# A one-core decoder trunk: overflow table and spill list moved into the expert loop, first experts in loop order

## What is computed

```python
def hier_moe(x, w_rg, b_rg, w_re, b_re, w_e1, w_e3, w_e2):
    g_idx = jnp.argmax(g_logits, axis=-1)                      # 1 of 4 groups
    top_v, top_i = lax.top_k(e_sel, TOP_K)                     # 2 of 8 experts in it
    top_w = jax.nn.softmax(top_v, axis=-1) * g_gate
    ...
        a = jnp.einsum('nd,edf->nef', xf, w_e1[g])
        b = jnp.einsum('nd,edf->nef', xf, w_e3[g])
        hid = jax.nn.silu(a) * b * gates[:, g, :, None]
        y = y + jnp.einsum('nef,efd->nd', hid, w_e2[g])
```

## Time and profile before

| | |
|---|---|
| median of 3 runs | 1172.28 us (1171.71 to 1172.39) |
| the profiled execution: own time | 1172.48 us |
| the profiled execution: span from first to last instruction | 1170.7 us |
| mean granted TensorE clock over the span | 0.954 of full |
| PE matmul busy | 1059.8 us, 91% |
| DVE, ACT, POOL busy | 645.6, 448.4, 196.9 us |
| moved by DMA | 203.04 MB |

### The profile page before, as it was taken

The page is one execution under the profiler, slowest core; times in us unless marked ns, Lnnn a source line. Parts: engine busy times, 40 slices in busy tenths (PEclk is TensorE's granted clock), DMA queues, the critical chain, the costliest instruction groups (busy, mean ns, idle before and its releaser), DMA issues. The chain is left out here.

```text
span 1170.7 us, 14132 instructions
## 1 busy us (share of the span) xinstructions
PE 1059.8 (91%) x5307; PEld 857.2 (73%) x5307; DVE 645.6 (55%) x1208; ACT 448.4 (38%) x777; POOL 196.9 (17%) x144
## 2 busy tenths in 40 slices
PE   2899999798999999998875999957999999999966
PEld 2899998697887799994542878745777777777722
DVE  5823735225644720004644115777888888888527
ACT  4522101204322522122421102255677777777413
POOL 3401211100000212100000300205422222222100
PEclk9999999999999999999986999967999999999978
DMA  9501111225000631106206101159999999999275
GB/s 331 146 19 36 40 55 36 90 73 200 11 1 30 227 140 54 37 8 280 108 1 257 67 1 73 55 192 386 340 382 392 379 386 394 371 400 363 89 303 185
DMA packets 55019, 203.04 MB, mean 173 GB/s; under 512 B 10534, under 2 KB 19231, under 8 KB 41383
## 3 DMA queue, kind: packets, MB, share of 16 engines
q1 hardware_dynamic: 44167, 181.61, 42.2%
q0 software_dynamic: 10784, 20.52, 4.8%
HBM read 189.52 MB, written 28.36 MB: 186 GB/s over the span
## 5 line engine op out<-in xcount | busy, mean ns | idle before, releaser
L500 PE MATMUL bank<-regA_r,regW_r 128*128 128x352 f32 (+1 forms) x456 | 149.6, 328 | 0.0
L499 PE MATMUL bank<-regA_r,regW_r 128*128 128x352 f32 (+1 forms) x456 | 149.3, 327 | 0.0
L498 PE MATMUL bank<-expert_w_r,regS_r 128*128 128x512 f32 x256 | 105.6, 413 | 2.6 <-DVE regS_r L2113 2.6
L334 POOL TENSOR_TENSOR regW_r<-regW,regW_r 128x1024 fp32r<-128x1024 f32 x19 | 47.2, 2487 | 330.5 <-ACT regW_r L328 330.5
L1416 ACT ACTIVATE regY_r<-expert_w 128x1024 fp32r<-128x1024 f32 x88 | 91.6, 1061 | 3.6 <-DMA expert_w<-in_we 3.6
L498 PE MATMUL bank<-regY_r,regW_r 128*128 128x352 f32 (+1 forms) x264 | 87.9, 333 | 0.5 <-ACT regB L1134 0.5
L2096 DVE TENSOR_TENSOR expert_w_r<-expert_w,regY_r 128x1024 fp32r<-128x1024 f32 x69 | 82.7, 1218 | 7.7 <-ACT regY_r L1416 7.7
L499 PEld LDWEIGHTS bank<-regA_r,regW_r 128*128 128x128 f32 x456 | 86.4, 190 | 0.4
L500 PEld LDWEIGHTS bank<-regA_r,regW_r 128*128 128x128 f32 x456 | 86.0, 189 | 0.0
L500 PE MATMUL bank<-regY_r,regA_r 128*128 128x512 f32 (+1 forms) x216 | 84.3, 390 | 0.0
L499 PE MATMUL bank<-regY_r,regB_r 128*128 128x512 f32 (+1 forms) x216 | 84.2, 390 | 0.0
(11 more groups left out here) (332 smaller groups left out, 2348.8 us busy)
## 6 DMA issues: line engine op xcount, KB each, us to landing
expert_w<-in_we SPq DMA_DIRECT2D x96, 1024.0 KB, 8.1
regW<-in_wbc SPq DMA_DIRECT2D x11, 512.0 KB, 3.6
regA<-in_kct SPq DMA_DIRECT2D x5, 1024.0 KB, 6.6
regY<-in_cache_mem_v SPq DMA_DIRECT2D x5, 1024.0 KB, 9.3
regS<-in_x_prompt SPq DMA_DIRECT2D x8, 512.0 KB, 9.0
regY<-in_xt SPq DMA_DIRECT2D x8, 512.0 KB, 8.5
regX<-in_x_prompt SPq DMA_DIRECT2D x8, 512.0 KB, 6.5
regW<-in_wq SPq DMA_DIRECT2D x8, 512.0 KB, 3.5
```

The lines of the kernel that those rows point to most:

```text
L334: eng.tensor_tensor(lo, raw, hi.bitcast(F32), ALU.subtract).then_inc(w_lo[name], 1)
L498: nc.tensor.matmul(out, stays[0], moves[1], start=first, stop=False)
L499: nc.tensor.matmul(out, stays[1], moves[0], start=False, stop=False)
L500: ins = nc.tensor.matmul(out, stays[0], moves[0], start=False, stop=last)
```

## The change

Seven edits, all around the start of the expert loop. (1) `place_in_table(0)` leaves tile 4, (1) and (2) leave the place behind `idx`; the three run at the ends of experts 5, 8 and 11 on DVE. (2) POOL's 18 table writes go two by two into experts 12 to 20. (3) `spill_list()` is cut into six pieces, at the ends of experts 16 to 26; `gates()` goes from expert 2 to 14. Their scratch moves to tiles that the loop doesn't overwrite. (4) On PE, `tokens(1)` is issued in the middle of `ab(0)`. (5) ACT rounds the down weights of expert 0 ahead of the tokens of expert 1. (6) A SiLU of one column is put behind the two Exp of the gates, so that the table for SiLU is loaded there. (7) SP issues piece 4 ahead of its wait, and then waits for three gathers instead of two.

```diff
-            def ab(e):
+            def ab(e, midway=None):
...
+                    if c == 2 and midway is not None:
+                        midway()
...
             for e in range(NE):
-                ab(e)
-                if e == 0:
-                    tokens(1)
+                ab(e, (lambda: tokens(1)) if e == 0 else None)
...
-            for p in range(2, 4):
+            for p in range(2, 5):
                 part_load(p)
-            for s in range(2):
-                sp.wait_ge(m_g[s], 16)
-            for p in range(4, 3 * NE):
+            sp.wait_ge(m_g[1], 16)
+            sp.wait_ge(m_g[0], 32)
+            for p in range(5, 3 * NE):
                 part_load(p)
...
+            nc.scalar.activation(small[:, 2:3], small[:, 0:1], ACT.Silu)
...
             for e in range(2):
                 act.wait_ge(m_tx, e + 1)
                 for q in range(2):
                     token_hi(e, q)
+                if e == 0:
+                    part_to_hi("down", 0, 0)
...
-                if t == 4:
-                    place_in_table(0)
...
-            place_in_table(1)
-            place_in_table(2)
...
-                if e == 0:
-                    spill_list()
-                if e == 2:
+                if e in (5, 8, 11):
+                    place_in_table((e - 5) // 3)
+                if e == 14:
                     gates()
+                if e == 16:
+                    spill_counts()
+                if e == 18:
+                    spill_ends((1, 2))
+                if e == 20:
+                    spill_ends((4, 8, 16))
+                if e == 22:
+                    spill_experts()
+                if e == 24:
+                    spill_before()
+                if e == 26:
+                    spill_columns()
...
-            g.wait_ge(s_plc, 1)
-            for t in range(GT):
-                for c in range(2):
-                    place_rows(t, c)
...
-            for t in range(GT, NT):
-                if t % GT == 0:
-                    g.wait_ge(s_plc, t // GT + 1)
-                for c in range(2):
-                    place_rows(t, c)
             for e in range(NE):
                 if e + 4 < NE:
                     rows_in(e + 4)
                 if e >= 1:
                     rows_out(e - 1)
+                if 12 <= e < 12 + NT:
+                    g.wait_ge(s_plc, (e - 12) // GT + 1)
+                    for c in range(2):
+                        place_rows(e - 12, c)
```

## The result

The changed kernel took **1161.38 us**, the median of 4 executions (1156.52 to 1162.57), against 1172.3 (1171.71 to 1172.39) for the kernel before beside it: ratio 0.990, 95% interval 0.9872 to 0.9929. In the course of the study more executions came together, on several chips: 10 of the changed kernel with a median of 1160.5 (1156.17 to 1162.57), and 40 of the kernel before with 1172.3 (1168.08 to 1177.39), 11.8 apart. The forecast was 1161.1, a gain of 11.2.

The account below looks back on a forecast made before the run. PE, busy for 91% of the span, was taken as the bound, with only waits and slow clock to win. Terms 1.08 + 1.26 + 2.10 + 0.84 + 2.41 + 1.89 + 1.60 make 11.2; 1172.3 less that is 1161.1 us, range 1159 to 1163.5.

Parts of the forecast that it names:

- Edit 1, router, 1.08: Router of tile 5: without the table piece beside tile 4, PE's wait goes, winning 1.08 us, at least 0.
- Edit 1, `token_lo(0)`, 1.26: Before the first up product: earlier low halves let PE start at 790.8 instead of 792.06, winning 1.26 us.
- Edits 4 and 5, 2.10: At `tokens(2)`: with `tokens(1)` inside `ab(0)`, PE's wait for `token_lo` goes, winning 2.10 us.
- Edit 6, 0.84: At `hidden(0)`: loading SiLU's table early wins 0.84 of the 1.08 us wait; 0.24 stays.
- Clock, 2.41 and 1.60: Over `ab(1)` and `ab(2)`: without the waits ahead the clock should not fall, winning 2.41 and 1.60 us.
- Edit 3, 1.89: At `hidden(1)`: with the spill list out of DVE's way, PE's wait for `hid(1)` goes, winning 1.89 us.
- The loop at 0: In the expert loop: the moved DVE pieces and POOL table writes fit into slack and cost PE 0 us.
- Loads late: First experts: late weight loads or gather 3 stop PE once or twice by 1 to 2 us; gain 7, chance 0.20.
- Table writes: In the loop: 18 table writes cost the DMA engines 4.9 us; if that reached PE, gain 6.3; chance 0.07.
- loop bound by DMA: In the loop: DMA engines already bind, PE only by coincidence; 2.2 us slower, 1174.5 us; chance 0.04.
- DVE one for one: In the loop: DVE's moved pieces reach PE in full, 11.2 less 11.5, no change at 1172.6 us; chance 0.03.
- SiLU's load not hidden: Before the first `token_hi`: a table load of twice 1.28 us passes ACT's idle time by 0.5; 1161.6 us; chance 0.03.

Follow-up runs that it names:

- the experiment with the late load: Changed kernel without the early one-column SiLU, so SiLU's table loads before the loop's first SiLU again: 1159.43 us, ratio 0.9885 to the kernel before.
- 2.64 in expert 16: PE's wait in the changed kernel with all six spill-list pieces together at the end of expert 16: 1163.97 us, ratio 0.9921 to the kernel before.

## Why the prediction was right, and where it was not

The forecast held: 1161.1 against 1161.38, inside the likeliest case's own range of 1159 to 1163.5. That it is right to 0.3 us is partly luck, for ten executions span 6.4 us, and by the starts of the same instructions these two traces are 12.6 us apart (1.19, 11.36 and 0.01), 0.7 of it by when the clock rose in `ab(0)`. Its steps held unevenly.

- **Edit 1, router, 1.08: right.** The wait is gone, and back at 1.09 when the piece is put back. The part to `tokens(0)` became 1.19 shorter (48.07 to 46.88), which contains also the loss of 0.51 below; the wait is 1.08 of it, and a last router that is 0.3 us quicker in this execution is most of the rest.
- **Edit 1, `token_lo(0)`, 1.26: its term right, its net too high.** From `tokens(0)` to the first product PE took 4.54 before (792.06 less 787.52) and 3.35 now, 1.19. What I said was lost for nothing, that DVE starts its long low halves earlier, in fact costs: they run beside POOL's issue of gather 0, and `tokens(0)` comes 6.07 behind the last list matmul instead of 5.56 (787.52 less 781.96). Net some 0.7. The experiments with pieces behind `idx` give back 0.37 and 0.35 of these 0.51; what the rest is stays open.
- **Edits 4 and 5, 2.10: right**, by the experiment with PE's order of before, which undoes edit 4; edit 5 was not undone by itself.
- **Edit 6, 0.84: the step that failed.** I read that the load "stands between the end of `ab(0)` and `hid(0)`" and gave its price to the edit that moves it. In the trace of before it began at 803.21 only because ACT was held by the halves of `tokens(1)`, and even there DVE stood idle for no more than 0.47 us for the SiLU behind it:

```profile
804.92 0.42 DVE L2117 TENSOR_TENSOR regW<-regY,bank 128x256 f32<-128x256 f32 x1 [0.47 <-ACT regY L1432]
```

  So by that row the edit alone could have won 0.47 at most. The wait was won without it, by the other edits; the sum was right because they were in the change. Edits 4 and 5 do it together (the experiment with the late load), and edits 5 and 6 do too (PE's order of before); which would do it alone isn't shown. It was worth 1.08 and not 0.84: `hidden(0)` starts 1.09 us behind `tokens(2)`, near the forecast 1.03, against 2.17 before (805.40 less 803.23). I had taken 0.24, counted from the start of PE's next work, off a wait of 1.08 that is counted from the end of the transposes. The Trainium skill (ScalarE: Activation LUTs, What ACT_TABLE_LOAD costs) adds 1.38 us of drain to each load. Both traces disagree: the one-column SiLU begins at 782.86, 0.01 us behind the load's end, and so does the SiLU of before (804.50 against 804.49).
- **Clock, 2.41 and 1.60: right in size.** Both falls are gone (`ab(1)` takes 5.56 us and `ab(2)` 5.57), and each returned with the wait ahead of it: 1.4 us behind 2.10 of waiting, 2.3 behind 4.26. A wait alone doesn't bring the fall, though: behind 2.64 in expert 16 there was none. The first phase, which I said I couldn't see, came out 0.7 us better in this execution: half clock for 4.0 us of `ab(0)` (787.00 to 791.01) instead of 5.3. `ab(0)` and `tokens(1)` take 8.37 together, against 9.07 before without the waits (8.03 and 1.04), and 9.04 to 9.13 in four other kernels of the new order.
- **Edit 3, 1.89: right for the sum, too small as the edit's worth.** Left in place, the list costs 4.26 and 2.3 of clock in the new order, by the experiment. Terms read from the trace of before are the worth of an edit only while the others don't move its neighbours.
- **The terms for `tokens(0)` to `tokens(4)`** (1.26, 2.10, 0.84, 2.41, 1.89, 1.60) make 10.1; measured 11.36. Of the excess 0.7 is that phase of the clock in `ab(0)`, 0.24 the term for `hidden(0)`, 0.16 `hidden(1)` (3.98 behind `tokens(3)` instead of 6.03, where I had 1.89), and 0.2 the two pairs of transposes of `hidden`, slow before.
- **The loop at 0: right.** 284.23 and 284.22 us.

The rivals. *Loads late*: pieces landed 4.8 to 16.5 us behind their issues at 789.8 to 792.4, ACT waited 0.91 and 0.43, and PE not at all; right that pieces come late, false in the price. *Table writes* and *loop bound by DMA*: false, since leaving the writes out gained nothing (342.85 us without them, 342.80 with them) and landings that differ by 1.2 us changed nothing. My estimate of 0.27 us a write came from a single stretch of 10 us; no run shows what a write costs the DMA engines. That PE stood still for part of that stretch doesn't explain its fewer bytes, for the engines' share was 0.98. The Trainium skill (DMA: Bandwidth & Descriptors, Specifications) wants at least 512 B in a transfer for full rate; no run here contradicts it, but 18 times 128 such rows, in a loop that moves about 94 MB in 240 us, cost PE nothing measurable. *DVE one for one*: false for pieces up to 1.75 us, and for one of 6.3 too, of which 2.64 comes through (expert 16). *SiLU's load not hidden*: false.

Left open: why the last stretch differs (59.3 and 58.6 us; the first 32 matmuls behind its long DMA wait took 16.87 in one and 16.34 in the other, and the wait 11.26 and 11.07), where the change touches nothing; what sets when the clock rises in `ab(0)`; and what the last 0.15 us are by which gather 0 comes later.

## What to carry to other kernels

Read what an instruction waited *behind* before you give its time to the edit that moves it: an expensive instruction between two others may be there only because its engine was held, and goes away with the holder. A chain of waits is one object: take them all out, for a list left in place costs more once the others are gone. Look at the clock behind each wait: its fall cost as much as the wait in one place (2.41 us behind 2.10 and 1.08) and nothing in another (behind 2.64). In a loop that one engine fills, odd work on another is free up to that engine's slack for each consumer, so cut it to pieces below the slack. And compare kernels by the starts of the same instructions, since the spread of whole executions can be as large as the term in question; but a stretch that begins at half clock has a spread of its own, 0.76 us here.

## What I had not expected of the hardware

- **Long DVE operations can slow POOL's issue of an indirect transfer.** Gathers 0 and 1 were issued in 1.05 and 1.01 us before, and in 1.10 and 1.01 in the kernel with two pieces behind `idx`, where DVE runs operations of some 0.17 us beside them; in 1.51 and 1.88 where DVE runs 1024-column subtractions. With one piece the first issue, beside short operations, took 1.10, and the second, beside long ones, 1.68. Not each long operation does it: in the changed kernel the issue at 796.68 took 1.00 though a 1024-column subtraction began at 796.93. The mechanism is not shown.
- **A table load isn't held by the wait of the instruction behind it**: in the kernel with the late load it ran at 796.18 while its SiLU waited until 797.82.
- **Matmuls of no use bring the clock up ahead of the work**, and the time is kept: 2.44 us for sixteen of them (granted clock 1.00 over `ab(0)` instead of 0.76).
- **The clock doesn't fall behind every wait, and the length of the wait alone doesn't decide it**: it fell behind 2.10 us of waiting with PE's order of before and stayed at 1.00 behind 2.64 in expert 16.
